# Seven-product pairs in the second expert product: weight sums finished by accumulating transfers, and twenty pairs per layer in place of sixteen

## What is computed

```python
def peer_ffn(x, norm_ffn, w_query, sub_keys, expert_down, expert_up):   # cut
    xn = rmsnorm(x, norm_ffn)
    ...                                                  # idx: picked experts, g: their gates
    act = gelu(einsum('btd,bthkd->bthk', xi, expert_down[idx]))
    return einsum('bthk,bthkd->btd', g * act, expert_up[idx])
```

## Time and profile before

| | us |
|---|---|
| median of 3 runs (2059.19 to 2060.71) | 2059.5 |
| profiled execution | 2064.05 |
| its span, first to last instruction | 2062.2 |
| TensorE busy in it | 2041.3 |
| VectorE / ScalarE / GpSimd busy in it | 1639.3 / 1356.3 / 373.5 |

### The profile page before, as it was taken

The page is one execution under the profiler, slowest core; times in us unless marked ns, Lnnn a source line. Parts: engine busy times, 40 slices in busy tenths (PEclk is TensorE's granted clock), DMA queues, the critical chain, the costliest instruction groups (busy, mean ns, idle before and its releaser), DMA issues.

```text
span 2062.2 us, 31647 instructions
## 1 busy us (share of the span) xinstructions
PE 2041.3 (99%) x11776; PEld 1749.0 (85%) x11776; DVE 1639.3 (79%) x2971; ACT 1356.3 (66%) x2303; POOL 373.5 (18%) x183
## 2 busy tenths in 40 slices
PE   8999999999999999999999999999999999999998
PEld 7788988888888888887888888888888888888888
DVE  7968988889869999877589888899689998743456
ACT  6665688878756666566646888777566666544674
POOL 1448800000000000012378100000000000045341
PEclk9999999999999999999999999999999999999999
DMA  6455855555566566664357655555656555676444
GB/s 231 153 156 168 238 171 169 173 165 167 171 190 203 190 213 202 206 210 143 120 167 222 192 169 168 170 174 167 191 179 208 205 194 188 225 217 197 130 157 139
DMA packets 108461, 376.26 MB, mean 182 GB/s; under 512 B 12372, under 2 KB 17908, under 8 KB 107412
## 3 DMA queue, kind: packets, MB, share of 16 engines
q1 hardware_dynamic: 107444, 369.00, 56.8%
q0 software_dynamic: 864, 5.24, 1.2%
HBM read 367.87 MB, written 1.08 MB: 179 GB/s over the span
## 4 chain that ended last, share of the span: by engine, by line
PE 92%; DVE 5%; ACT 1%; DMA 1%; issue 1%; POOL 0%; SPq 0%; DVEq 0%; ACTq 0%
PE ps L211 29%; PE ps L212 14%; PE ps L205 14%; PE ps L207 14%; PE ps L206 14%; PE ps L1126 3%; DVE WL L192 1%; DMA raw<-in_l_up_dram 1%; PE ps L1105 1%; DVE arena L818 1%; PE ps L1149 1%; DVE arena L815 0%; PE ps L2394 0%; PE ps L2418 0%; PE ps L1152 0%
## 5 line engine op out<-in xcount | busy, mean ns | idle before, releaser
L186 ACT ACTIVATE WH<-raw 128x1024 fp32r<-128x1024 f32 (+1 forms) x680 | 701.7, 1036 | 304.5 <-PE ps L207 186.7
L211 PE MATMUL ps<-X,WH 128*128 128x512 f32 x2528 | 895.9, 398 | 0.1
L212 PE MATMUL ps<-X,WL 128*128 128x256 f32 x2528 | 707.0, 280 | 0.0
L192 DVE TENSOR_TENSOR WL<-raw,WH 128x1024 fp32r<-128x1024 f32 (+1 forms) x554 | 661.9, 1197 | 39.0 <-ACT WH L186 38.2
L198 POOL TENSOR_TENSOR WL<-raw,WH 128x1024 fp32r<-128x1024 f32 x126 | 319.1, 2556 | 1572.6 <-ACT WH L186 1570.5
L211 PEld LDWEIGHTS ps<-X,WH 128*128 128x128 f32 x2528 | 474.0, 188 | 107.8 <-issue 0.6
L212 PEld LDWEIGHTS ps<-X,WL 128*128 128x128 f32 x2528 | 477.2, 189 | 0.1
L205 PE MATMUL ps<-WH,X 128*128 128x512 f32 (+1 forms) x784 | 310.4, 396 | 1.6 <-DVE X L417 0.9
L207 PE MATMUL ps<-WH,X 128*128 128x512 f32 (+1 forms) x784 | 305.4, 390 | 0.0
L206 PE MATMUL ps<-WL,X 128*128 128x512 f32 (+1 forms) x784 | 305.1, 389 | 0.0
L205 PEld LDWEIGHTS ps<-WH,X 128*128 128x128 f32 x784 | 147.5, 188 | 36.9 <-issue 4.5
(11 more groups left out here) (355 smaller groups left out, 2640.2 us busy)
## 6 DMA issues: line engine op xcount, KB each, us to landing
raw<-in_l_down_dram SPq DMA_DIRECT2D x256, 512.0 KB, 3.6
raw<-in_l_up_dram SPq DMA_DIRECT2D x256, 512.0 KB, 4.2
raw<-in_l_wq_dram SPq DMA_DIRECT2D x32, 512.0 KB, 3.5
raw<-in_w_qk_dram SPq DMA_DIRECT2D x24, 512.0 KB, 3.7
raw<-in_w_gates_dram SPq DMA_DIRECT2D x24, 512.0 KB, 3.5
raw<-in_l_nat_dram SPq DMA_DIRECT2D x16, 512.0 KB, 3.5
raw<-in_l_wout_dram SPq DMA_DIRECT2D x16, 512.0 KB, 3.6
raw<-in_l_win_dram SPq DMA_DIRECT2D x16, 512.0 KB, 4.0
```

The source lines that it names most:

```text
L186: a.activation(WH[:, i % NW, 0:w], raw[:, i % NW, 0:w], ACT.Copy).then_inc(w_high, 1)
L192: v.tensor_tensor(WL[:, i % NW, 0:w], raw[:, i % NW, 0:w], WH[:, i % NW, 0:w], ALU.subtract).then_inc(w_low_v, 1)
L211: t.matmul(PS[:, bank, :], w[0], X2[:, k, :, :].rearrange("p w t -> p (w t)"), start=first, stop=False)
L212: return t.matmul(PS[:, bank, 0:256], w[1], X2[:, k, 0, :], start=False, stop=last)
```

## The change

`SEVEN` lists twenty pairs instead of sixteen. The four weight sums are now made so: ScalarE copies the first chunk's two blocks with the sign turned (`seven_weights13`), VectorE makes one difference (`seven_weights2`) and, after the G low part, a second one (`seven_weights4`); then GpSimd issues a transfer that reads both chunks of the pair once more from the chip's main memory and adds them to `SUM_T` (1 MB, `accum_op=ALU.add`). It waits for the fourth sum and for the transfer before it. The high part of all four sums is one ScalarE copy 2048 wide, which waits for the transfer, the low part one VectorE subtract 2048 wide. `SUM_T` has two homes, the row sums and the G parts more homes than before. The distances `c - 2p` are now: rows -3, row high part -2, row low part -1, weight sums -2, high part 4, low part 5, products 6. One of the five row sums (`SUM_D`) falls away.

The diff, cut (count and home tables, and the renaming of the final adds, are left out):

```diff
-        SEVEN = tuple(range(10, 56, 3))
+        SEVEN = (7, 11, 15, 17, 20, 22, 24, 27, 29, 31, 34, 36, 38, 41, 43, 45, 48, 50, 52, 55)
+        ROWS_AT, ROWS_LOW_AT, WEIGHTS_AT, WEIGHTS_HIGH_AT, WEIGHTS_LOW_AT, SUMS_AT = -3, -1, -2, 4, 5, 6
...
             if i - NW in IN_SEVEN:
                 l, m, j = IN_SEVEN[i - NW]
-                s.wait_ge(seven_v, seven_count(l, m, ("weights2", "weights4")[j]))
+                s.wait_ge(seven_v, seven_v_at(l, m, "weights2"))
+                if j == 0:
+                    s.wait_ge(seven_a, seven_a_at(l, m, "weights13"))
...
-        LOW_T = SPLIT[:, 0:4, :]
+        LOW_T = SPLIT[:, 6:10, :]
+        SUM_HOMES = (ar(0, 4, 512), 4), (ar(5120, 4, 512), 14)
...
-                t.wait_ge(seven_v, seven_count(l, m, "weights_low0"))
-                for n, (bank, part) in enumerate(((1, 1), (2, 3), (3, 2), (6, None))):
-                    if n == 2:
-                        t.wait_ge(seven_v, seven_count(l, m, "weights_low1"))
+                t.wait_ge(seven_v, seven_v_at(l, m, "weights_low"))
+                for n, bank, part in ((1, 1, 1), (3, 2, 3), (0, 3, 2), (2, 6, None)):
...
-                if c % 2 == 0 and c // 2 - 2 in SEVEN:
-                    seven_sums(c // 2 - 2)
+                if c % 2 == 0 and (c - SUMS_AT) // 2 in SEVEN:
+                    seven_sums((c - SUMS_AT) // 2)
...
+        def seven_weights13(a, l, c):
+            for m, p in enumerate(SEVEN):
+                if c == 2 * p + WEIGHTS_AT:
+                    i, q = bases(l)[2] + 2 * p, before(OF_SUM_T, m)
+                    a.wait_ge(raw_in[i % NW], 16 * (i // NW + 1))
+                    if q is None:
+                        a.wait_ge(g_low, 64 * l + SUM_HOMES[OF_SUM_T[m]][1])
+                    else:
+                        a.wait_ge(seven_v, seven_v_at(l, q, "weights_low"))
+                    a.activation(sum_t(m)[:, 1:4:2, :], raw[:, i % NW, :].rearrange("p (b n) -> p b n", b=2), ACT.Copy,
+                                 scale=-1.0).then_inc(seven_a, 1)
...
-                if r in (-1, 0):
-                    a.wait_ge(seven_done, u)
-                    a.wait_ge(seven_v, seven_count(l, m, "weights4" if r == 0 else "weights13"))
-                    w = slice(2 * r + 2, 2 * r + 4) if r == 0 else slice(0, 2)
-                    a.activation(HIGH_T[:, w, :], SUM_T[:, w, :], ACT.Copy).then_inc(seven_a, 1)
+                if c == 2 * p + WEIGHTS_HIGH_AT:
+                    a.wait_ge(early_sum, 16 * (N_SUMS * l + 3 + m + 1))
+                    a.wait_ge(seven_done, len(SEVEN) * l + m)
+                    a.activation(HIGH_T.rearrange("p a b -> p (a b)"), sum_t(m).rearrange("p a b -> p (a b)"),
+                                 ACT.Copy).then_inc(seven_a, 1)
...
             for c in range(124):
+                seven_weights13(a, l, c)
                 high(a, up + c + 3)
...
+        def seven_weights2(v, l, m):
+            i = bases(l)[2] + 2 * SEVEN[m]
+            v.wait_ge(raw_in[(i + 1) % NW], 16 * ((i + 1) // NW + 1))
+            if before(OF_SUM_T, m) is not None:
+                v.wait_ge(seven_v, seven_v_at(l, before(OF_SUM_T, m), "weights_low"))
+            v.tensor_tensor(sum_t(m)[:, 0, :], raw[:, (i + 1) % NW, 512:1024], raw[:, i % NW, 512:1024],
+                            ALU.subtract).then_inc(seven_v, 1)
+
+        def seven_weights4(v, l, m):
+            w = sum_t(m)
+            v.wait_ge(seven_a, seven_a_at(l, m, "weights13"))
+            v.wait_ge(seven_v, seven_v_at(l, m, "weights2"))
+            v.tensor_tensor(w[:, 2, :], w[:, 1, :], w[:, 0, :], ALU.subtract).then_inc(seven_v, 1)
+
+        def seven_weights_low(v, l, m):
+            v.wait_ge(seven_a, seven_a_at(l, m, "weights_high"))
+            v.tensor_tensor(LOW_T, sum_t(m), HIGH_T, ALU.subtract).then_inc(seven_v, 1)
...
+            for m, p in reversed(tuple(enumerate(SEVEN))):
+                if c == 2 * p + ROWS_AT:
+                    seven_rows(v, l, m)
+                if c == 2 * p + ROWS_LOW_AT:
+                    seven_rows_low(v, l, m)
+                if c == 2 * p + WEIGHTS_LOW_AT:
+                    seven_weights_low(v, l, m)
...
                 low_v(v, up + c + 2)
-                if c // 2 + 1 in SEVEN:
-                    seven_vector(v, l, c)
+                seven_vector(v, l, c)
                 if c % 2 == 0:
-                    split_g_vector(v, l, c // 2 + 1)
-                if c // 2 + 1 not in SEVEN:
-                    seven_vector(v, l, c)
+                    p = c // 2 + 1
+                    if p in SEVEN:
+                        seven_weights2(v, l, SEVEN.index(p))
+                    split_g_vector(v, l, p)
+                    if p in SEVEN:
+                        seven_weights4(v, l, SEVEN.index(p))
...
+                if c - 146 in [2 * p for p in SEVEN]:
+                    m, p = SEVEN.index((c - 146) // 2), (c - 146) // 2
+                    g.wait_ge(seven_v, seven_v_at(l, m, "weights4"))
+                    g.wait_ge(early_sum, 16 * (N_SUMS * l + 3 + m))
+                    g.dma_start(sum_t(m).rearrange("p (j h) n -> p j (h n)", j=2),
+                                d[f"l{l}_up"][2 * p:2 * p + 2].rearrange("j p n -> p j n"),
+                                accum_op=ALU.add).then_inc(early_sum, 16)
```

## The result

The changed kernel takes 2131.1 us (median of 6 runs, 2128.08 to 2134.87), the kernel before on the same chip 2059.8 (6 runs, 2058.78 to 2062.41): a ratio of 1.0347, 95% interval 1.0336 to 1.0357. It is slower, as forecast, but by 71.4 us where 29.3 were forecast, and outside the range of 2070 to 2115.

The account below looks back on a forecast made before the run. TensorE, busy 99% of the span, was taken as the bound. Products -5.4, chain waits +34.7 and traffic 0 sum to +29.3 us: 2093.4 from the profiled 2064.05, or 2088.8 as a median, range 2070 to 2115.

Parts of the forecast that it names:

- Products, -5.4: TensorE, both up stages: four more seven-product pairs per layer, one product less each at 0.678 us, 5.4 us saved.
- The chain of 5.61 us, +34.7: Up stages: high part, low part, products one step apart; 5.61 us until products can start, TensorE waits 34.7 us in all.
- two-apart pairs: Eleven of 20 pairs with a seven pair two later: TensorE waits 0.86 us, or 1.07 us in five of them.
- three-apart ones: Six pairs with the next seven pair three later: chain of 7.24 us against 6.10 us of products, 1.14 us of waiting.
- The new homes of the G parts: Up stages: G parts' new buffer places released no later than the ordinary high part's chunk, so this move is free.
- Traffic at 0: Effect of 40 added 1 MB transfers on loads: between a 5.1 us gain and a 52 us loss, taken as 0.
- the row of 243 to 253 us: Nearest profile row for the traffic: transfer engines full beside such a transfer, TensorE still busy 10 of 10 us.
- the rival that hung on it: Transfer engines full: the bound from about 5.4 us per transfer, loads land late, up to 2141 us; chance 0.16.
- Loads up to 2.7 us late: Loads issued beside a transfer land after 6.0 to 8.0 us, against a median of 4.3 in the seven-product stretch.
- Sums late: Rival: transfers landing past 14.8 us add their lateness 34 to 40 times; at 16 us, 2134 us; chance 0.04.
- Products in time: Rival: low part ready at e(2p+6), when TensorE finishes chunk 2p+6; TensorE sets the pace, 2054.1 or 2049.0 us; chance 0.11.
- the signs set down for "wrong": Up stages: no TensorE gaps and a period of 36, or gaps from raw blocks or accumulating queue, loads landing after 7 us.

Follow-up runs that it names:

- the kernel with cut transfers and the better order: Changed kernel, transfers cut to 64 columns, start's wait gone, wide copy and wide subtract ahead of their step's weight chunk: 2054.6 us.
- without traffic, the order alone: Changed kernel with every accumulating transfer cut from 1 MB to 32 KB, all waits and engine order kept: 2094.7 us, ratio 1.0160.
- the old order: Kernel before, its order untouched, plus 18 accumulating 1 MB transfers per layer into memory nobody reads: 2135.0 us, ratio 1.0347.
- long transfers: Kernel before plus 18 accumulating transfers per layer into memory nobody reads, every second cut to 64 columns, the others 1 MB: 2104.0 us.
- short ones: Kernel before plus 18 accumulating transfers per layer into memory nobody reads, each one block of 512 KB: 2083.7 us.

## Why the prediction was right in sign and wrong in size

- **Products, -5.4.** Right: in the kernel with cut transfers and the better order the layer 0 stage is 2.6 us shorter. (The 6.0 us that this kernel is faster in all also hold layer 1's old loss.)
- **The chain of 5.61 us, +34.7.** The mechanism, the 17 places per layer and their pattern were right. The two-apart pairs waited 0.70 and 1.00 instead of 0.86 and 1.07, the three-apart ones 1.03 instead of 1.14: 31.0 us without traffic. The two widths were 2287 and 1902 ns (2280 and 1930 forecast). The working left out the slower matmuls after each wait (about 0.15 us, 34 times: 5 us), the next point (3.3) and that layer 1 loses its own 4 us no more beside such waits: 31.0 + 5 + 3.3 - 5.4 - 4 = 30. That is the distance of the two profiled executions, 29.6; the medians are 33.7 apart because the profiled one of the kernel before was a long one. Layer 1's loss is 3.7 us by the lengths of the two stages on TensorE (338.7 and 335.0), not 5.1: the prediction read it off VectorE's starts.
- **"The new homes of the G parts are all released at or before the chunk that the ordinary high part waits for anyway."** Wrong for pair 0. Before, pair 0 waited for no slot; now every pair without a predecessor waits until the last down chunk is done. It cost about 3 us.
- **Traffic at 0.** This is the step that failed. It cost 36.4 us here and 74 in the old order (36 transfers). The price was chosen between -5.1 and +52 by the row of 243 to 253 us, in which the engines are full and TensorE is not late. That was the wrong row to be nearest to: ten microseconds beside one transfer are no longer than what four slots of `raw` can cover (by our estimate four chunks of 335/128 = 2.6 us in the up stage), and say nothing of a stage that must keep its rate for 300 us. The engine time per transfer was forecast well: 46.1% x 11 = 5.1 us, and the point of full engines 5.4; measured 37.2% x 300 / 20 = 5.6. By the rival that hung on it the forecast would have been up to 2141, and it had 0.16. But that rival's mechanism, total engine time, is not quite what decided either: at equal fullness long transfers cost 43 us and short ones 25. What decided is that an accumulating 1 MB is under way for 11.5 us: beside it raw blocks come later than four slots can cover, TensorE stops, and after the longest stops its clock falls. In the trace of the change that is 13.7 us of longer waits for the 2048-wide subtract (44.7 against 31.0 without traffic), 12.7 of waits for L1649 and 7.6 of lower clock, 34 together.
- **"Loads up to 2.7 us late."** The longest landing in the stretch is 10.1 us (6.1 before), 4 us late. One place shows this from load to TensorE. ScalarE, VectorE and TensorE near 644 us (timelines, one engine after the other):

```profile
644.12 1.06 ACT L202 ACTIVATE WH<-raw 128x1024 fp32r<-128x1024 f32 x1 [4.77 <-DMA raw<-in_l_up_dram]
646.05 1.06 ACT L202 ACTIVATE WH<-raw 128x1024 fp32r<-128x1024 f32 x1 [0.87 <-DMA raw<-in_l_up_dram]
647.01 0.61 ACT L1393 ACTIVATE GH<-arena 128x512 fp32r<-128x512 f32 x1
...
645.21 1.22 DVE L208 TENSOR_TENSOR WL<-raw,WH 128x1024 fp32r<-128x1024 f32 x1 [4.00 <-ACT WH L202]
647.66 0.69 DVE L1649 TENSOR_TENSOR GL<-arena,GH 128x512 fp32r<-128x512 f32 x1 [1.22 <-ACT GH L1393]
...
646.11 0.39 PE L223 MATMUL ps<-WH,X 128*128 128x512 f32 x1
648.50 0.47 PE L221 MATMUL ps<-WH,GH 128*128 128x512 f32 x1 [2.01 <-DVE GL L1649]
```

ScalarE stands idle for 4.77 us until a raw block has landed. The high part of G is queued behind two late chunks, the low part of G behind that, and TensorE starts 2.39 us after its last matmul. The profile names a VectorE subtract as what TensorE waited for; followed back it is a load.

- **Sums late (0.04).** Did not happen in the change (landing at most 13.0 us, the copy idle 0.0), but it is the next limit: in two pieces the sums were late and cost 62 us.
- **The rival "Products in time" (0.11).** It was argued against from the handovers, rightly for this order; swapping two neighbours on each engine was enough to make it come true. A version that beats the kernel before would need the sums finished for under 6 us in all. Neither way tried here does that; making them on GpSimd from plain copies was not tried, since by the homes in the code no 8 KB per partition are free for the copies before pair 24.

What the trace was to show came: the wait after chunk 2p+6 put down to the 2048-wide subtract, VectorE's share down (263.7 to 238.5 of 300). Seven pairs took 40.9 us (starts of transfers at 695.38 and 858.98, four periods), not 39; and the signs set down for "wrong", raw blocks and late loads, were there too.

## What to carry to other kernels

Price a background transfer in engine time per megabyte and in the time for which one is under way, and set the second against what the foreground's buffers hold, over the whole stage; a short stretch in which nothing was late is no price. An accumulating transfer cost nearly twice the engine time of a copy here, and halving its length saved more than its bytes would say, as long as nobody waits for it. When two engines' queues carry a chain with no slack, look first at the order within a step: the same two operations ahead of their neighbours were worth nearly 40 us, 3 of them the start's wait, as long as the transfers were cut; beside whole ones the same order lost 20 (2150.6 against 2131.1).

## What the runs showed of the hardware

**Accumulating from main memory.** 5.7 us of all engines for a transfer of 1 MB and 11.5 us to landing, against 3.0 and 6.0 for a plain copy of the same bytes on the same queue. The Trainium skill ("DMA: Bandwidth & Descriptors", section "Rules for kernel authors") says that the accumulate reads its destination and writes it later; the nearly doubled engine time is what one would expect of that, but no run here shows the reads themselves.

**The clock after a wait.** After the wait at 648.50 us (2.39 us between starts) TensorE's granted clock falls to half, the lower of its two levels (1.2 of 2.4 GHz), and is back some 3 us later. Stretches ahead of it, in it and behind (columns as in the earlier trace rows), and its matmuls, 0.63 us long and 0.43 apart instead of 0.39 and 0.23:

```profile
640.00:646.00 6.00, 6.00 (x28) 4.99 (x27) 2.00 (x3) 1.06 (x1) 0.00 (x0) 1.00 1.03 332
649.40:652.60 3.20, 3.20 (x9) 2.44 (x8) 3.17 (x7) 3.20 (x6) 0.00 (x0) 0.50 0.62 166
656.00:660.00 4.00, 4.00 (x20) 3.30 (x19) 2.76 (x5) 1.34 (x2) 0.73 (x1) 1.00 0.82 211
...
650.91 0.63 PE L222 MATMUL ps<-WL,GH 128*128 128x512 f32 x1
651.34 0.63 PE L223 MATMUL ps<-WH,GL 128*128 128x512 f32 x1
```

Eight or nine matmuls at 0.43 instead of 0.23 apart are 1.6 to 1.8 us, nearly as much as the wait itself. It happened five times in the two stages (losses of 2.16, 2.70, 2.44, 2.88 and 2.90 us before it), not after losses of 2.15 and 1.94 us in the same run (so the length of a wait alone does not decide it), and never after the 1 us waits of the order alone, whose mean clock was 1.000.
